# Mixer queues of a hybrid attention step in a new order, and the recurrence's norm gain folded into the output weights

## The reference, cut to what matters

```python
def merge(o_gla, gg, gla_norm, o_swa, w_o):
    B, H, T, DV = o_gla.shape
    og = rmsnorm(o_gla.transpose(0, 2, 1, 3), gla_norm).reshape(B, T, GLA_WIDTH) * jax.nn.silu(gg)
    osw = o_swa.transpose(0, 3, 1, 2, 4).reshape(B, T, SWA_WIDTH)
    return jnp.concatenate([og, osw], axis=-1) @ w_o
```

## Time and profile before

| what | value |
|---|---|
| median of 3 runs | 1686.18 us (1684.71 to 1688.66) |
| the profiled execution | 1684.21 us, span 1682.3 us |
| mean granted TensorE clock | 0.993 |
| PE busy | 1603.9 us (95%) |
| PEld busy | 1394.7 us (83%) |
| DVE busy | 1020.3 us (61%) |
| ACT busy | 673.6 us (40%) |
| POOL busy | 1016.3 us (60%) |

### The profile page before, as it was taken

The page is one execution under the profiler, slowest core; times in us unless marked ns, Lnnn a source line. Parts: engine busy times, 40 slices in busy tenths (PEclk is TensorE's granted clock), DMA queues, the critical chain, the costliest instruction groups (busy, mean ns, idle before and its releaser), DMA issues.

```text
span 1682.3 us, 31906 instructions
## 1 busy us (share of the span) xinstructions
PE 1603.9 (95%) x11618; PEld 1394.7 (83%) x11618; DVE 1020.3 (61%) x1584; ACT 673.6 (40%) x1192; POOL 1016.3 (60%) x758
## 2 busy tenths in 40 slices
PE   4999999998999888899999999999999999999997
PEld 1998778996777766788888998989978899998996
DVE  2713565666676669455866566575695545545468
ACT  2514224225444345312354444444535444444441
POOL 1711554654574789002487787777898667667682
PEclk9999999999999999999999999999999999999999
DMA  9254565659555455333661322313235132231322
GB/s 331 92 159 137 196 210 175 224 179 263 160 171 158 158 158 152 108 130 142 200 224 57 100 75 75 100 51 99 88 114 174 51 100 72 78 100 50 99 64 100
DMA packets 211450, 225.93 MB, mean 134 GB/s; under 512 B 52752, under 2 KB 171664, under 8 KB 208144
## 3 DMA queue, kind: packets, MB, share of 16 engines
q1 hardware_dynamic: 209248, 224.46, 41.6%
q10 hardware_dynamic: 2096, 0.02, 0.1%
HBM read 177.22 MB, written 47.24 MB: 133 GB/s over the span
## 4 chain that ended last, share of the span: by engine, by line
PE 43%; POOL 4%; DVE 2%; issue 1%; ACT 0%; DMA 0%; SPq 0%; DVEq 0%; ACTq 0%; POOLq 0%
PE ff_banks L3095 8%; PE ff_banks L3096 8%; PE ff_banks L3097 8%; PE ff_banks L3068 7%; PE ff_banks L3070 7%; PE ff_banks L3069 7%; POOL h_whi L2734 1%; POOL h_xop L2332 1%; POOL h_wlo L2746 1%; POOL h_whi L2741 1%; DVE ff_tmp L2935 1%; DVE ff_acc L2925 0%; DMA ff_hb<-in_w_ff 0%; DVE ff_acc L2919 0%; DVE ff_acc L2892 0%
## 5 line engine op out<-in xcount | busy, mean ns | idle before, releaser
L3068 PE MATMUL ff_banks<-h_xop,h_whi 128*128 128x320 f32 x888 | 275.2, 310 | 5.8 <-DVE wo_raw L2872 3.1
L3070 PE MATMUL ff_banks<-h_xop,h_whi 128*128 128x320 f32 x888 | 274.4, 309 | 0.0
L3069 PE MATMUL ff_banks<-h_xop,h_whi 128*128 128x320 f32 x888 | 274.4, 309 | 0.0
L2892 DVE TENSOR_TENSOR ff_acc<-ff_acc,ff_banks 128x512 f32<-128x512 f32 x294 | 199.0, 681 | 99.2 <-PE ff_banks L3097 99.2
L3095 PE MATMUL ff_banks<-h_wlo 128*128 128x512 f32 x600 | 234.3, 390 | 1.6 <-DVE ff_acc L2892 0.8
L3097 PE MATMUL ff_banks<-h_wlo 128*128 128x512 f32 x600 | 233.5, 389 | 0.0
L2734 POOL TENSOR_TENSOR h_whi<-mid_raw,h_whi 128x512 fp32r<-128x512 f32 x149 | 207.2, 1406 | 1.4 <-ACT h_whi L2586 1.4
L2746 POOL TENSOR_TENSOR h_wlo<-mid_raw,h_wlo 128x320 fp32r<-128x320 f32 x128 | 116.6, 913 | 129.6 <-ACT mid_raw L2623 129.6
L3068 PEld LDWEIGHTS ff_banks<-h_xop,h_whi 128*128 128x128 f32 x888 | 166.7, 188 | 9.5 <-issue 4.8
L3069 PEld LDWEIGHTS ff_banks<-h_xop,h_whi 128*128 128x128 f32 x888 | 166.7, 188 | 1.1
L3070 PEld LDWEIGHTS ff_banks<-h_xop,h_whi 128*128 128x128 f32 x888 | 166.7, 188 | 0.0
(11 more groups left out here) (306 smaller groups left out, 3774.2 us busy)
## 6 DMA issues: line engine op xcount, KB each, us to landing
mid_raw<-in_w_ff SPq DMA_DIRECT2D x124, 512.0 KB, 4.3
mid_raw<-in_w_ada SPq DMA_DIRECT2D x18, 1024.0 KB, 7.2
early_room<-qk_by_channel SPq DMA_DIRECT2D x20, 512.0 KB, 4.1
proj<-prj_stage SPq DMA_DIRECT2D x60, 152.0 KB, 1.9
mid_raw<-in_w_in SPq DMA_DIRECT2D x6, 1216.0 KB, 7.2
early_room<-in_w_ada SPq DMA_DIRECT2D x6, 1024.0 KB, 10.9
decays<-early_room SPq DMA_DIRECT2D x8, 640.0 KB, 4.5
early_room<-decays SPq DMA_DIRECT2D x20, 256.0 KB, 2.9
```

Source lines behind the costliest of these rows:

```text
L2892: dve.tensor_tensor(acc[:, p, at], acc[:, p, at], down[n % RING], ALU.add).then_inc(added, 1)
L3068: pe.matmul(out, w_hi[:, k], x_hi[:, k], start=(k == 0), stop=False)
L3069: pe.matmul(out, w_hi[:, k], x_lo[:, k], start=False, stop=False)
L3070: mm = pe.matmul(out, w_lo[:, k], x_hi[:, k], start=False, stop=(k == KH - 1))
```

## The change

- `score[:, 0]` no longer takes the transposed queries (except those of unit 0): they go to `rec.ps[:, 1]`, one of the recurrence's score banks, in odd slots and behind the recurrence; `pe_scores` then waits for `low_queries`.
- `query_at`, `ctx_at`, `loc_at`, `turn_at` are filled by another rule; a turn has a side of its own. The beats are written out as one list per engine. In VectorE's, `rec.dve_state(1)` stands ahead of the wait for the tables, the two mask copies come last, and the memset of `qlow` moves to GpSimd. SyncE stores step 0 and loads step 3 first.
- Order within a slot on TensorE: side 0, scores, `pe_turned` (the transposes split off `pe_scores`), side 1, queries, recurrence scores, values, outputs. On ScalarE `act_output` moves to the next slot's head, the decays and the output tile ahead of `outputs(u)`. On GpSimd `pool_mid` moves ahead of `pool_state`, which moves a slot behind.
- An output tile: ScalarE also adds the one (Identity with bias) and squares; GpSimd keeps the sum, the gate, the root, the norm and the last product, the latter four two slots behind the sum. SyncE loads two slots ahead, VectorE's sum of squares moves to two slots behind.
- The gain is loaded once per partition (two rows of 64) and multiplied into the first half of the rows of the output weights, on ScalarE in the copy and on VectorE in the rest; both instructions are cut into two halves. The product with the gain per tile (L1102) goes.
- The state update of both halves is written to the same columns, so that `dve_new` is one instruction over 128 partitions. `Keys` copies once instead of twice.

```diff
     def act(self, act, n):
         act.wait_ge(self.loaded[n % 2], 48 * (n // 2) + 48)
         if n >= 2:
-            act.wait_ge(self.factor_ready, n - 1)
-        act.activation(self.tanh[:, n % 2], self.gg[:, n % 2], ACT.Tanh, scale=0.5).then_inc(self.tanh_ready, 1)
+            act.wait_ge(self.si_ready, n - 1)
+        if n:
+            act.wait_ge(self.factor_ready, n)
+        act.activation(self.tanh[:, :], self.gg[:, n % 2], ACT.Tanh, scale=0.5).then_inc(self.tanh_ready, 1)
+        act.wait_ge(self.tanh_ready, n + 1)
+        act.activation(self.factor[:, n % 2], self.tanh[:, :], ACT.Identity, bias=1.0).then_inc(self.factor_ready, 1)
+
+    def act_square(self, act, n):
+        act.wait_ge(self.o_ready, n + 1)
+        if n:
+            act.wait_ge(self.ssq_ready, n)
+        act.activation(self.sq[:, :], self.o[:, n % 2], ACT.Square).then_inc(self.sq_ready, 1)
 
     def pool_sum(self, pool, n):
         j = n % 2
         pool.wait_ge(self.loaded[j], 48 * (n // 2) + 48)
-        pool.tensor_tensor(self.o[:, :], self.of[:, j], self.ob[:, j], ALU.add).then_inc(self.o_ready, 1)
-        pool.wait_ge(self.o_ready, n + 1)
-        if n:
-            pool.wait_ge(self.ssq_ready, n)
-        pool.tensor_tensor(self.sq[:, :], self.o[:, :], self.o[:, :], ALU.mult).then_inc(self.sq_ready, 1)
-        pool.wait_ge(self.tanh_ready, n + 1)
-        pool.tensor_tensor(self.factor[:, :], self.tanh[:, j], self.one[:, 0:1].broadcast_to([P, GW]), ALU.add).then_inc(self.factor_ready, 1)
-        pool.wait_ge(self.factor_ready, n + 1)
-        pool.tensor_tensor(self.si[:, :], self.gg[:, j], self.factor[:, :], ALU.mult).then_inc(self.si_ready, 1)
+        if n >= 2:
+            pool.wait_ge(self.on_ready, n - 1)
+        pool.tensor_tensor(self.o[:, j], self.of[:, j], self.ob[:, j], ALU.add).then_inc(self.o_ready, 1)
 
     def dve(self, dve, n):
...
-        pool.tensor_tensor(self.heads(self.og[:, :]), self.heads(self.on[:, :]), self.gain[:, :].unsqueeze(1).broadcast_to([P, H, DH]),
-                           ALU.mult).then_inc(self.og_ready, 1)
...
+        act.wait_ge(self.gain_ready, 1)
+        half = GW // P
+        act.activation(self.whi[:, 0:half, self.columns(n)], self.raw[:, n % 2, 0:half], ACT.Copy, scale=self.gain[:, 0:1]).then_inc(self.whi_ready, 1)
+        act.activation(self.whi[:, half:2 * half, self.columns(n)], self.raw[:, n % 2, half:2 * half], ACT.Copy).then_inc(self.whi_ready, 1)
...
+        dve.wait_ge(self.whi_ready, 2 * n + 1)
+        dve.scalar_tensor_tensor(self.wlo[:, first, self.columns(n)], self.raw[:, n % 2, first], self.gain[:, 0:1],
+                                 hi_view(self.whi)[:, first, self.columns(n)], ALU.mult, ALU.subtract).then_inc(self.wlo_ready, 1)
+        dve.wait_ge(self.whi_ready, 2 * n + 2)
+        dve.tensor_tensor(self.wlo[:, second, self.columns(n)], self.raw[:, n % 2, second], hi_view(self.whi)[:, second, self.columns(n)],
+                          ALU.subtract).then_inc(self.wlo_ready, 1)
...
-    def pe_scores(self, pe, x):
+    def pe_turned(self, pe, x):
         i, d, t = self.place(x)
         pe.wait_ge(self.ke_ready, x + 1)
         if x:
-            pe.wait_ge(self.new_ready, 2 * x)
+            pe.wait_ge(self.new_ready, x)
         for b in range(self.HP):
             tr = pe.transpose(self.ps[:, 2, b * P:(b + 1) * P], self.ke[:, d, b], self.keep["ident"])
         tr.then_inc(self.tr_ready, 1)
+
+    def pe_scores(self, pe, x):
+        i, d, t = self.place(x)
...
-        for half in range(2):
-            rows = slice(half * DH, (half + 1) * DH)
-            upd = self.ps[rows, 2].rearrange("p (b c) -> p b c", c=P)[:, :, half * DH:(half + 1) * DH]
-            dve.tensor_tensor(self.new[rows], upd, self.decayed(d, t, rows, 2), ALU.mult).then_inc(self.new_ready, 1)
+        dve.tensor_tensor(self.new[:, :, :], self.update(), self.decayed(d, t, slice(0, P), 2), ALU.mult).then_inc(self.new_ready, 1)
...
-        act.activation(self.keys_of(self.kdup, slice(0, P), n), self.turned(slice(0, P), n), ACT.Copy).then_inc(self.dup_ready, 1)
-        act.activation(self.keys_of(self.khl, slice(0, DH), n), self.turned(slice(0, DH), n), ACT.Copy).then_inc(self.hl_ready, 1)
+        act.activation(self.keys_of(self.khl, slice(0, P), n), self.turned(slice(0, P), n), ACT.Copy).then_inc(self.hl_ready, 1)
...
+        spare = [w for w in range(SLOTS) if w % 2 or w >= REC_END]
+        query_at, turn_at, ctx_at, loc_at = {}, {}, {}, {}
+        todo = []
         for u in range(1, U):
             for p in range(2):
-                if u < LONG:
-                    ctx_at[free.pop(0)] = (u, p)
-                loc_at[free.pop(0)] = (u, p)
-            at = free.pop(0)
-            if u + 1 < U:
-                while u + 1 >= QRING and at[0] < done_slot[u + 1 - QRING] - 1:
-                    at = free.pop(0)
-                query_at[at] = u + 1
-            turn_at[at] = u
-            assert at[0] < first_slot[u]
+                if (u, p) == (2, 0):
+                    todo.append(("turn", 1, 0))
+                if u < LONG and (u, p) != (1, 0):
+                    todo.append(("ctx", u, p))
+                if u > 2 and p == (0 if u < LONG else 1):
+                    todo.append(("turn", u - 1, 0))
+                todo.append(("loc", u, p))
+        todo.append(("turn", U - 1, 0))
+        asked = {u: -2 for u in range(2)}
+        for w in range(SLOTS):
+            for side in range(2):
+                if todo and asked.get(todo[0][1], SLOTS) + 2 - side <= w:
+                    kind, u, p = todo.pop(0)
+                    {"ctx": ctx_at, "loc": loc_at, "turn": turn_at}[kind][w, side] = (u, p)
+                    assert kind != "turn" or w < first_slot[u], (u, w, first_slot[u])
+            u = len(asked)
+            if w in spare and u < U and (u < QRING or last_scores[u - QRING] <= w):
+                query_at[w] = u
+                asked[u] = w
...
+        def turned_queries(u):
+
+            return score[:, 0] if u < LEAD else rec.ps[:, 1]
...
+                rec.pool_scaled(pool, 2)
                 for n in range(2, keys.N):
                     keys.pool(pool, n)
-                for x in range(2, FIRST + 2):
-                    rec.pool_scaled(pool, x)
-                glo.pool_gain(pool)
+                rec.pool_scaled(pool, FIRST)
+                pool.wait_ge(rec.qe_ready, FIRST + 1)
+                pool.memset(qlow[DH:96, :, :, :].bitcast(F32), 0.0).then_inc(cleared, 1)
+                pool.wait_ge(cleared, 1)
                 rec.pool_masked(pool)
                 rec.pool_mid(pool, FIRST)
+                rec.pool_scaled(pool, FIRST + 1)
+                glo.pool_gain(pool)
                 for w in range(SLOTS):
-                    if w in outputs_at:
-                        x = outputs_at[w]
+                    if w - 1 in outputs_at:
+                        x = outputs_at[w - 1]
                         rec.pool_state(pool, x)
-                        if x + 1 < X:
-                            rec.pool_mid(pool, x + 1)
                         if x + 2 < X:
                             rec.pool_scaled(pool, x + 2)
+                    if w in outputs_at and outputs_at[w] + 1 < X:
+                        rec.pool_mid(pool, outputs_at[w] + 1)
                     if w in glo_at:
                         glo.pool_sum(pool, glo_at[w])
...
-                    if w - 1 in glo_at:
-                        glo.pool_scale(pool, glo_at[w - 1])
+                    if w - 2 in glo_at:
+                        glo.pool_scale(pool, glo_at[w - 2])
...
-                    wait_room(("query", u))
+                    if u < LEAD:
+                        keys.pe_room_free(pe, 3)
+                    else:
+                        pe.wait_ge(qlow_ready, u)
+                        pe.wait_ge(rec.at_ready, rec_steps(query_slot[u]))
                     for m in range(HG):
-                        mm = pe.transpose(score[:, 0, m * P:(m + 1) * P], xq[:, n % 2, kv * HG + m].rearrange("p c d -> p (c d)"), keep["ident"])
+                        mm = pe.transpose(turned_queries(u)[:, m * P:(m + 1) * P], xq[:, n % 2, kv * HG + m].rearrange("p c d -> p (c d)"), keep["ident"])
...
+                    late = 1 <= w <= SLOTS and crossing(w)
+                    if w == 0:
+                        rec.pe_turned(pe, FIRST)
+                        pe.wait_ge(qlow_ready, 2)
+                        rec.pe_scores(pe, FIRST)
+                        raw_context(1, 0)
+                    else:
+                        ahead((w, 0))
+                    if w == 1:
+                        pe.wait_ge(tables, 5)
                     if w < SLOTS:
                         scores(2 * w)
                         scores(2 * w + 1)
-                    ahead((w, 0))
-                    late = 1 <= w <= SLOTS and crossing(w)
+                    if w == 0:
+                        ahead((w, 0))
+                    elif w in scores_at:
```

(34 more changed lines are left out.)

320 lines of the change are left out of this document (156 added, 164 removed).

## The result

The changed kernel takes 1695.5 us (median of four, 1693.5 to 1697.9) against 1686.8 (1684.7 to 1688.7) for the kernel before, run in turn with it: a ratio of 1.0052, 95% interval 1.0033 to 1.0071. It is half a per cent slower, where 1657.8 us (1642 to 1675) was predicted.

What follows compares the result with a forecast made beforehand. TensorE was taken to bound the mixer's middle, with three engines holding each other up in turn behind it. Start -3.5, middle -15.4 and tail -9.5 sum to -28.4, so 1686.2 - 28.4 = 1657.8 us, range 1642 to 1675.

Steps and rivals of the forecast that it cites:

- The start, -3.5: Before slot 0: less work in VectorE's queue ends a 3.50 us stop and helps the clock a little, -3.5 us.
- The middle, -15.4: The 17 recurrence steps in 34 slots: waits of TensorE removed, less something given back, -15.4 us in sum.
- Queries in another bank: Middle: queries leave the score bank, so raw scores no longer wait for VectorE's subtraction, -4.8 us.
- `pe_outputs` behind `values`: Middle: the outputs' first product follows 64-column work instead of 128x128 work and pays no wait, -3.6 us.
- the pair that I had priced at zero to 3.6: Middle, even slots: the 64-row output product meeting 64-column values directly, 0 to 3.6 us, counted as zero.
- the output tiles' -3.9: Middle: GpSimd's shorter output-tile work removes a 2.88 us stop and about 1.0 ahead of the local product, -3.9 us.
- The +4 given back: Middle: side 1's second product can wait for the second maximum in some 13 slots, +4 us, bounds 0 and 8.8.
- peaks get a side of their own: -5.1: Middle: turned peaks stop sharing a side, removing 2.4 us of waits for the spread and 2.7 for the turn.
- The tail, -9.5: The 24 slots without recurrence: TensorE gets back part of 13.6 us, limited by VectorE; -9.5, bounds -4 and -13.6.
- the first rival: Whole mixer: VectorE is the bound behind TensorE, so waits return elsewhere; only -12 us, so 1674; chance 0.18.
- The slower rival: Eight close output tiles: ScalarE's square waits for GpSimd's sum, 44 us on top, so 1702; chance 0.07.
- The clock: TensorE's granted clock at 1.00 from 420 us to the mixer's end; worth -2.0 us in the middle.

Runs made afterwards that it cites:

- e7: e5 with GpSimd making recurrence step 2's products ahead of the memset of the constant keys: 1672.1 us, ratio 0.9918 to the kernel before.
- e10: e9 with the halves of the output weights' rest in neighbouring slots, and e7's order ahead of slot 0: 1671.4 us, ratio 0.9895 to the kernel before.
- e3: The changed kernel with turns of the peaks on side 1 of a slot only: 1681.2 us, ratio 0.9973 to the kernel before.
- e6: e5 with seven of the eight output-weight pieces one slot later, so none stands in a slot with queries: 1669.1 us, ratio 0.9900 to the kernel before.
- e1: The changed kernel with VectorE taking the queries' rest in the slot of their transposes from slot 34 on: 1681.8 us, ratio 0.9964 to the kernel before.
- e5: The changed kernel with the edits of e1 and e3 together: 1673.1 us, ratio 0.9928 to the kernel before.
- e11: e6 with GpSimd's four wide operations covering 64 of 512 channels for output tiles 5 to 9, the rest left out: 1669.0 us, ratio 0.9890.
- e9: e6 with VectorE's sum of squares behind the slot's maxima and the queries' rest: 1672.7 us, ratio 0.9910 to the kernel before.
- e12: e6 with the output-weight pieces in slots 37, 40, 43, 46, 47, 50, 51, 52, where GpSimd has little: 1671.6 us, ratio 0.9909.
- e8: The kernel before, its queues and slots kept, with the gain in the output weights and the one and the square on ScalarE: 1701.5 us, ratio 1.0085.

## Why the prediction was wrong

- **The start, -3.5: failed.** The stop of 3.50 us is gone, but GpSimd's chain is the next late one: in the lead its keys' copy waits 2.3 us for a DMA, the memset of the constant keys takes 3.09 from 400.90 on, and step 2's product comes only at 404.07. I had followed GpSimd from its key copies to the memset of `qlow`, which I put at 409 to 411 and which ended at 414.1, and had not asked what waited behind the other memset. That this chain holds the lead is read from one trace and not shown: with its products ahead of the memset the lead was 31.2 us in `e7` and 34.3 in `e10`. In the nine variants on the new queues that leave GpSimd's order there alone, the lead took 28.4 to 33.1 us, so the 1.4 more in the kernel after is no finding by itself.
- **The middle, -15.4: right in size, -11.0 came.** Queries in another bank: 4.8 to 0. `pe_outputs` behind `values`: L1301 pays 0.0, so -3.6 held; L1288 pays 4.0, where the same line (L1272 then) had 2.8. These 1.2 more are not the pair that I had priced at zero to 3.6. In 13 of its 16 steps L1288 stands directly behind the raw scores, 128x128 work, and waits 0.24 to 0.36 us, where L1272 stood behind the transposes and waited 0.17 in each. In two steps it stands behind the 64-column values, and waits for nothing; in the others the values follow it with a gap of 0.12 us where I looked. So the pair costs nothing that shows. The Trainium skill (TensorEngine Tiling (Array Packing), section "Key Properties") has a change of tiling mode drain TensorE: the rows behind 128x128 work agree, and between the values and L1288, of 64 columns and of 64 rows, no such wait is seen. What I hadn't counted: the idle time ahead of the values themselves fell from 9.6 to 5.6 us. Of the output tiles' -3.9 the "issue" ahead of the local product shows most, 4.4 before and 0.7 after. The +4 given back came as 1.0 us for the second maximum (L2033). Of the two waits of the earlier trace rows, ScalarE's for the load of `gg` is gone; VectorE's for the squares, which ScalarE makes now, is 6.4 us in four over the mixer, 3.7 in the longest.
- **In the middle, "peaks get a side of their own: -5.1" failed.** A side of their own isn't a slot of their own: with the turn on side 0 the local product of side 1 needs the bank's spread, and L2076 released 7.0 instead of L2012's 2.4, and the turn stood 6.4, of which L1784's 2.7 was to be saved. `e3` took this away: the middle is 18.1 us shorter than before there, and 16.8 in `e6`. Some 2 us of that is work put off: TensorE loads 45 raw-score weights in the tail of `e6` and 40 in that of before, at 0.35 to 0.5 us of matmul each.
- **The tail, -9.5: failed, it was +17.6.** I had priced that VectorE can't follow, by its busy share, and had left the order of its queue out. The text says of the middle that nothing is lost "unless VectorE or ScalarE is over a microsecond behind"; in the tail I never asked where `low_queries(w - 1)` stands. It stands behind the whole of the slot before, the weights' piece included, and that piece waits for ScalarE (16.3 us in the tail). Where I had taken away 7.9 us for L1960 and 3.3 for L2012, both waits grew by 4.4; most of the rest went with the lower clock. `e1` removed the first and nothing else: -12.1. `e3`'s edit took the spread's part, 2.6 more with it (`e5`, 89.0).
- **Even mended, the tail is no shorter than before** (85 to 90 us against 86.1). The idle time ahead of the two raw scores is 6.9 + 8.0 = 14.9 us before, 6.2 + 8.2 = 14.4 in `e6`, 14.6 in `e11`: the same sum with other releasers, the maxima (L2049 and the "issue" behind VectorE's queue) and more of the spread (5.0 in `e6` against 3.3) for L1960. That is the first rival, "the banks wait for maxima", in the tail alone, and it isn't VectorE's busy share that does it (56.6 of 85.0 us in `e11`), but, where I looked, pieces of work in its queue without a gap, such as the 6 us in the timeline of `e9`. No edit of one such place made the sum smaller: 18.7 in `e9`, 15.4 in `e10`, 14.6 in `e11`, 15.7 in `e12`. What would end it, I didn't find.
- **The slower rival** (ScalarE blocked by GpSimd's sum) gave 1702, for the wrong kernel: `e8` has it, and that it came out at 1701.5 is luck, since its waits are 7.3 us in four, not 5.5 in each tile, and a late lead is a third of its loss. That the changed kernel came out slower had a cause that no rival named.
- **The clock** was to be 1.00 from 420 on: 0.98 in the middle, 0.84 in the tail. Where stops went, it rose (0.91 in `e1` and `e3`, 0.92 in `e6`, 0.96 in `e11`). But `e9` and `e10`, with two stops of 3.9 to 4.5 us each, have 0.94, so the long stops alone don't set it. No run changed the clock alone.

By the marks, `e6` has -0.1 in the lead, -16.8 in the middle, +1.3 in the tail and begins 1.3 later: -14.3 of the 14.6 us that its span (1667.7) is shorter. Of the 28.4 predicted the middle's part was there, behind two orders.

## What to carry to other kernels

When an operation is moved, write down for each engine that it passes what stands ahead of it in that engine's queue in every stage of the schedule, not only in the one that bounds: a step that costs 0.7 us came 4 us late because an unrelated piece, waiting for a third engine, stood before it. A bank freed is worth what its next user gains, so follow the new occupant too. And a rebuild that comes out slower can be a gain with two orders wrong in it: cut the traces at marks of the work, find the stage that lost, and mend that alone.
